# Norm weights, positions and conv taps: five transposes on TensorE against two block transposes on VectorE

## The reference

```python
def rmsnorm(x, gain):
    xf = x.astype(jnp.float32)
    y = xf * lax.rsqrt(jnp.mean(xf * xf, axis=-1, keepdims=True) + EPS)
    return (y * gain.astype(jnp.float32)).astype(x.dtype)

def swiglu(x, w1, w3, w2):
    return (jax.nn.silu(x @ w1) * (x @ w3)) @ w2

# block 1
h = h + 0.5 * swiglu(rmsnorm(h, ffn1_norm), ffn1_w1, ffn1_w3, ffn1_w2)     # D_FF = 2816
u = rmsnorm(h, mix_norm);  proj = u @ w_in                                 # then pooling and retention
a = pool_mixer(u_pool, pool_w, pool_scale);  b = retention(q, k, v, g, ret_norm)
h = h + jnp.concatenate([a, b], axis=-1) @ w_out
h = h + 0.5 * swiglu(rmsnorm(h, ffn2_norm), ...);  x = rmsnorm(h, final_norm)
# block 2: rmsnorm (norm_mix), window and compressed attention (adds cmp_pos_k, cmp_pos_v to the keys
# and values), rmsnorm (norm_ffn), then a feed-forward whose 5632 inner columns go through a causal
# convolution over 3 tokens (conv_w, conv_b), then rmsnorm (norm_final)
```

## Time and profile before

| | |
|---|---|
| median of 3 runs | 834.4 us (834.33 to 834.74) |
| the profiled execution | 834.21 us, its span 832.4 us |
| TensorE busy | 823.4 us, 99% of the span |
| VectorE, ScalarE, GpSimd busy | 625.1, 439.5, 89.8 us (75%, 53%, 11%) |
| DMA, mean over the span | 189 GB/s |

### The profile page before, as it was taken

One profiled execution on the slowest core, in us unless ns is written; L12 is line 12 of the kernel. 1 busy time (PEld: TensorE's weight loads), 2 busy tenths in 40 slices (PEclk: granted clock), 3 DMA queues, 4 the chain that ended last, 5 costly groups with the idle time before them and its releaser, 6 DMA issues.

```text
span 832.4 us, 13214 instructions
## 1 busy us (share of the span) xinstructions
PE 823.4 (99%) x5041; PEld 711.0 (85%) x5041; DVE 625.1 (75%) x779; ACT 439.5 (53%) x559; POOL 89.8 (11%) x93
## 2 busy tenths in 40 slices
PE   9999999999999999999999999999999999999996
PEld 6888888888988888888888899878788988888895
DVE  5786766667977587667667779767874898998897
ACT  6555444546334554454444746566435556665664
POOL 0300000004450300000000317000003000000001
PEclk9999999999999999999999999999999999999999
DMA  8876566564844458756665594684545365466551
GB/s 260 304 239 213 188 194 204 170 201 151 254 153 151 152 185 259 246 194 201 198 205 152 130 243 125 175 259 150 177 157 181 118 204 200 151 206 216 183 176 52
DMA packets 115888, 157.69 MB, mean 189 GB/s; under 512 B 4445, under 2 KB 95997, under 8 KB 115725
## 3 DMA queue, kind: packets, MB, share of 16 engines
q1 hardware_dynamic: 113212, 150.56, 56.3%
q0 software_dynamic: 1392, 5.34, 1.9%
q10 hardware_dynamic: 1248, 1.32, 0.5%
HBM read 154.42 MB, written 1.07 MB: 187 GB/s over the span
## 4 chain that ended last, share of the span: by engine, by line
PE 96%; DVE 1%; DMA 1%; ACT 1%; issue 1%; POOL 0%; ACTq 0%; POOLq 0%; DVEq 0%
PE wk L1760 30%; PE acc L1882 20%; PE wk L1729 16%; PE wk L1768 16%; PE acc L1859 7%; PE acc L2173 1%; PE acc L1776 1%; PE wk L2209 1%; PE acc L1729 1%; DMA x<-in_x 1%; PE acc L2188 1%; PE wk L2246 0%; ACT w_hi L516 0%; PE acc L1895 0%; DVE w_lo L1061 0%
## 5 line engine op out<-in xcount | busy, mean ns | idle before, releaser
L1760 PE MATMUL wk<-xhl,w_hi 128*128 128x512 f32 x1104 | 268.9, 391 | 0.0
L1078 DVE TENSOR_TENSOR w_lo<-raw,w_hi 128x2048 fp32r<-128x2048 f32 x83 | 189.9, 2289 | 63.7 <-ACT w_hi L523 62.5
L1760 PEld LDWEIGHTS wk<-xhl,w_hi 128*128 128x128 f32 x1104 | 202.3, 188 | 39.3 <-issue 0.3
L523 ACT ACTIVATE w_hi<-raw 128x2048 fp32r<-128x2048 f32 x83 | 158.0, 1903 | 0.0
L1768 PEld LDWEIGHTS wk<-xhl,w_lo 128*128 128x128 f32 x1104 | 145.5, 191 | 8.0
L1768 PE MATMUL wk<-xhl,w_lo 128*128 128x256 f32 x1104 | 147.9, 282 | 0.0
L516 ACT ACTIVATE w_hi<-raw 128x2048 fp32r<-128x2048 f32 x51 | 97.0, 1911 | 53.7 <-PE wk L1729 28.4
L1061 DVE TENSOR_TENSOR w_lo<-raw,w_hi 128x2048 fp32r<-128x2048 f32 x44 | 101.3, 2302 | 24.9 <-ACT w_hi L516 24.7
L1882 PE MATMUL acc<-w_hi,hhl 128*128 128x512 f32 x480 | 119.4, 391 | 0.0
L1882 PEld LDWEIGHTS acc<-w_hi,hhl 128*128 128x128 f32 x480 | 88.2, 188 | 17.1
L1729 PE MATMUL wk<-xhl,w_hi 128*128 128x256 f32 x352 | 61.3, 286 | 0.0
(11 more groups left out here) (266 smaller groups left out, 977.9 us busy)
## 6 DMA issues: line engine op xcount, KB each, us to landing
raw<-in_ffn_w SPq DMA_DIRECT2D x64, 1024.0 KB, 5.3
raw<-in_w_in SPq DMA_DIRECT2D x24, 1024.0 KB, 7.2
raw<-in_w_ffn_in SPq DMA_DIRECT2D x22, 1024.0 KB, 5.0
raw<-in_w_ffn_out SPq DMA_DIRECT2D x11, 1024.0 KB, 4.9
raw<-in_w_out SPq DMA_DIRECT2D x8, 1024.0 KB, 4.9
arena<-bias_scratch POOLq DMA_DIRECT2D x4, 512.0 KB, 6.2
raw<-in_w_in SPq DMA_DIRECT2D x4, 512.0 KB, 7.0
raw<-in_cmp_w_k SPq DMA_DIRECT2D x2, 1024.0 KB, 5.5
```

The source lines that it names most:

```text
L523: nc.scalar.activation(w_hi[:, s], raw[:, s], ACT.Copy).then_inc(hi_done, 1)
L1078: nc.vector.tensor_tensor(w_lo[:, s], raw[:, s], w_hi[:, s].bitcast(F32), ALU.subtract) \
L1760: mm = nc.tensor.matmul(bank, wh[:, c, cols], xhl[:, c].rearrange("p n t -> p (n t)"), start=c == 0, stop=False, skip_group_check=True)
```

## The change

Four things:

1. `small_loads` on SyncE's queue loses its 14 small loads. GpSimd's queue gets them in quarters: 32 columns at a time and at most 32 rows, each to the partitions 32j to 32j+31 of `quarter_rows`, which GpSimd sets to zero first. That is 4 quarters of 10 vectors, and 4 quarters of 2 pieces (32 and 12 rows) of 4 taps: 72 loads of 4 to 32 rows of 128 bytes, 1056 rows in all. They stand on GpSimd's queue behind the table and `pool_w`, and ahead of the product of the two norm weights.
2. TensorE's five transposes and ScalarE's two copies go, with their waits.
3. VectorE turns the quarters in blocks of 32 by 32: one instruction over 96 columns to `vec`, one over 256 columns to `conv`. They stand in the last step of the first feed-forward, between the remainder of that step's last weight unit and `b_add`.
4. ScalarE waits for `vec_ready` ahead of the scaling that follows the first feed-forward. `conv` has 64 instead of 44 columns per tap.

```diff
@@ small_loads (SyncE)
-                for col, name in ((V_MIX, "mix_norm"), (V_FFN2, "ffn2_norm"), (V_MIX2, "norm_mix_2"),
-                                  (V_FFN3, "norm_ffn_2"), (V_POOL, "pool_scale"), (V_RET, "ret_norm")):
-                    v = rows8(a[name][0])
-                    sp.dma_start(vec_rows[col:col + v.shape[0], :], v).then_inc(vec_in, 16)
...
-                for j in range(3):
-                    sp.dma_start(conv_rows[:, j], rows8(a["conv_w_2"][0, j])).then_inc(conv_in, 16)
-                sp.dma_start(conv_rows[:, 3], rows8(a["conv_b_2"][0])).then_inc(conv_in, 16)
@@ ScalarE
+                if n == 1:
+                    act.wait_ge(vec_ready, 2)
                 for c in range(DC):
                     x_hi(c, n, gain)
...
-                    vectors()
@@ GpSimd
+            nc.gpsimd.memset(quarter_rows, 0.0).then_inc(rows_zero, 1)
...
             nc.gpsimd.dma_start(scratch, bias_rows).then_inc(bias_written, 16)
+            nc.gpsimd.dma_start(table, a["c_table"]).then_inc(table_in, 16)
+            nc.gpsimd.dma_start(pool_ws, a["pool_w"][0].rearrange("g k n -> k g n")).then_inc(pw_in, 16)
+
+            def quarters(at, rows):
+
+                n = rows.shape[0]
+                for r0 in range(0, n, 32):
+                    m, (block, first) = min(32, n - r0), divmod(at + r0, 32)
+                    for j in range(4):
+                        nc.gpsimd.dma_start(quarter_rows[32 * j + first:32 * j + first + m, 32 * block:32 * block + 32],
+                                            rows[r0:r0 + m, 32 * j:32 * j + 32]).then_inc(vec_in, 16)
+
+            pool.wait_ge(rows_zero, 1)
...
             pool.wait_ge(vec_ready, 2)
             nc.gpsimd.tensor_tensor(vec[:, V_BOTH:V_COLS], vec[:, V_FINAL:V_FINAL + DC], vec[:, V_MIX2:V_MIX2 + DC],
                                     ALU.mult).then_inc(both_gain, 1)
-            nc.gpsimd.dma_start(table, a["c_table"]).then_inc(table_in, 16)
-            nc.gpsimd.dma_start(pool_ws, a["pool_w"][0].rearrange("g k n -> k g n")).then_inc(pw_in, 16)
@@ VectorE, last step of ffn
                 lo(base + 3 * FI - 1)
+                if f == 0:
+                    dve.wait_ge(vec_in, 16 * VEC_LOADS)
+                    nc.vector.transpose(vec[:, 0:R_CONV], quarter_rows[:, 0:R_CONV]).then_inc(vec_ready, 1)
+                    nc.vector.transpose(conv[:].rearrange("p j f -> p (j f)"), quarter_rows[:, R_CONV:]) \
+                        .then_inc(vec_ready, 1)
                 b_part(FI - 1)
@@ TensorE
                     if spreads:
                         pe.wait_ge(rstd_ready, n + 1)
-                        pe.wait_ge(vec_ready, 2)
...
-                    turn_vectors()
```

More of the change, by code:

```diff
@@ L114 @@
 V_BOTH, V_COLS = 96, 104
+R_CONV, R_COLS = 96, 96 + 4 * 64
+VEC_LOADS = 4 * (10 + 2 * 4)
 C_ID, C_FOLD, C_VALC, C_BLK, C_COLS = 0, 128, 160, 190, 198
@@ L213, in build @@
         vec_rows = carve(8, P)
+        quarter_rows = carve(9, R_COLS)
         q_s, k_s = carve(0, HR, T), carve(4, HR, T)
@@ L237, in build @@
         bias_table = carve(57.5, NBUCKET)[0:16]
-        conv_rows = carve(58, 4, P)[0:44]
         bias = carve(0, 16, T)
@@ L264, in build @@
         wg_raw = work[:, 5, T:T + 192].rearrange("p (k n) -> p k n", k=DC)
-        conv = sb("conv", [P, 4, 44])
+        conv = sb("conv", [P, 4, 64])
         sink = sb("sink", [P, NHA])
@@ L307, in build @@
         const_set = sem("const_set")
-        vec_turned, vec_ready = sem("vec_turned"), sem("vec_ready")
+        rows_zero, vec_ready = sem("rows_zero"), sem("vec_ready")
         acc_ready, x_ready, turned, xh_ready, xl_ready, sq_ready = (
@@ L329, in build @@
             sem(n) for n in ("gate_tanh", "head_out", "head_hi", "head_lo"))
-        bias_in, conv_in, cw2_in, wg_in, sink_in = (
-            sem(n) for n in ("bias_in", "conv_in", "cw2_in", "wg_in", "sink_in"))
+        bias_in, cw2_in, wg_in, sink_in = (
+            sem(n) for n in ("bias_in", "cw2_in", "wg_in", "sink_in"))
         bias_set, bias_written, bias_ready = (sem(n) for n in ("bias_set", "bias_written", "bias_ready"))
@@ L619, in ffn @@
                 hi(base + 3 * FI + 1)
[L621 to L626, removed]
             for p in range(4):
@@ L933, in _ @@
             nc.gpsimd.dma_start(scratch, bias_rows).then_inc(bias_written, 16)
+            nc.gpsimd.dma_start(table, a["c_table"]).then_inc(table_in, 16)
[8 more added lines that the diff above has]
+            pool.wait_ge(rows_zero, 1)
+            for col, name in ((V_MIX, "mix_norm"), (V_FFN2, "ffn2_norm"), (V_MIX2, "norm_mix_2"),
+                              (V_FFN3, "norm_ffn_2"), (V_POOL, "pool_scale"), (V_RET, "ret_norm")):
+                quarters(col, rows8(a[name][0]))
+            for col, name in ((V_FINAL, "final_norm"), (V_FINAL2, "norm_final_2")):
+                quarters(col, rows8(a[name]))
+            for col, name in ((V_POSK, "cmp_pos_k_2"), (V_POSV, "cmp_pos_v_2")):
+                quarters(col, a[name][0].rearrange("(j s) d -> j (s d)", s=2))
+            for j in range(4):
+                quarters(R_CONV + 64 * j, rows8(a["conv_w_2"][0, j] if j < 3 else a["conv_b_2"][0]))
             pool.wait_ge(vec_ready, 2)
@@ L2017, in second_unit @@
                 return split_low(slot, 1, wk[:, 3])
[L2019 to L2027, removed]
             pe.wait_ge(const_set, 3)
```

## The result

The changed kernel takes 838.88 us (median of 5 runs, 838.78 to 839.19) against 834.4 us before (834.33 to 834.74): ratio 1.0051, 95% interval 1.004 to 1.0062. It is slower by 4.5 us, 0.5%. The prediction said 834.9 us, within 833.9 to 836.2. Its profiled execution has a span of 836.9 us. In all the sets of this document one execution, of the kernel with one added load, ran at a lower granted clock (0.75) and took 1018.3 us; it is in no comparison.

What follows compares the result with a forecast made beforehand. The prediction took TensorE's work and waits as the bound. Terms: 0 (transposes), 0 (ScalarE, SyncE, GpSimd, traffic) and 0.50 (VectorE) made +0.5 us, 834.7 from the profiled 834.21, or 834.9 against the median; range 833.9 to 836.2 us.

Steps and rivals of the forecast that it cites:

- What bounds the kernel: Whole program: TensorE, busy 823.4 of 832.4 us, so the total moves only with TensorE's work or its waits.
- the 0 for GpSimd in the sum: GpSimd's queue: issuing the 72 loads from about 30 us stays hidden and adds 0 us to the total.
- The transposes that go: TensorE between units 1 and 2, near 20 us: removal gains 0 us, bounds 0 and -0.45 us.
- Rival A: TensorE, unit 1 to unit 2: it recovers the transposes' 0.45 us, total 834.4 to 834.5 us; chance 8%.
- The block transposes: VectorE ahead of `b_add`, end of the first feed-forward: +0.50 us fully on the path, bounds 0.31 and 1.60 us.
- rival B: VectorE, end of the first feed-forward: a block transpose costs four passes, +1.6 us, total 836.0 us; chance 7%.
- The 72 loads on GpSimd's queue: GpSimd from about 30.2 us: issues take 37 to 62 us, hidden before VectorE needs them at 182.9; 0 us.
- rival C: VectorE's wait at 182.9 us: the quarters come too late; at 2.5 us a load, total 862 us; chance 4%.
- SyncE's queue: SyncE, near 10 to 16 us: unit 3's load goes out up to 6.4 us earlier, nobody waits; 0 us.
- rival D: Near 16 us: unit 3's load shares the DMA with unit 2's, up to +6.3 us, 834.9 to 841.2; chance 4%.

## Why the prediction was wrong

**What bounds the kernel: the failed step.** The prediction said that "The total moves only where TensorE's work changes, or where a wait of TensorE appears or goes". That holds as long as TensorE works, up to about 826 us. The execution ends with the last engine's closing drain, and GpSimd's had 832.2 - 830.0 = 2.2 us to spare before. The term that failed is the 0 for GpSimd in the sum. I counted what 72 loads cost where they are issued and where they are waited for, and not what they leave on the queue for the end: 72 x 0.082 = 5.9 us, of which 3.7 stood out. The kernel with the 72 loads alone and the one with the inserted drain show it: +3.8 us and -3.5 us. The rows for it existed in the trace of before, a drain of 2.35 us on GpSimd against 0.007 on SyncE. The busy times and the timeline leave drains out; they stand in the list of the instructions of the program's last line, which the prediction did not use. They would have shown the drain and its room; what one load more costs could not be read there, since there was only the one number of loads, 20.

**The transposes that go, 0 us: right.** The wait for the remainder took their place. I expected unit 2 at 20.6 to 20.7 us behind 0.4 us of idle time; in the profile after, unit 2 landed later and it is

```profile
21.04 1.68 PEld L1770 LDWEIGHTS wk<-xhl,w_hi 128*128 128x128 f32 x8 [0.99 <-issue]
```

Rival A falls by the run with five idle transposes.

**The block transposes, +0.50 us: right.** 0.27 and 0.40 us each, from start to start 183.27 - 183.08 = 0.19 and 183.60 - 183.27 = 0.33, together 0.52. The timeline after, against the earlier trace rows:

```profile
183.08 0.27 DVE L1220 STREAM_TRANSPOSE vec<-arena 128x96 f32<-128x96 f32 x1
183.27 0.40 DVE L1221 STREAM_TRANSPOSE conv<-arena 128x256 f32<-128x256 f32 x1
183.60 0.65 DVE L1164 TENSOR_TENSOR work<-wk,work 128x512 f32<-128x512 f32 x1
...
187.75 0.19 PEld L1869 LDWEIGHTS acc<-w_hi,mhl 128*128 128x128 f32 x1 [0.86 <-issue]
```

The idle time ahead of the closing unit grew from 0.38 to 0.86, so 0.48 us reached TensorE. A transpose streams like an elementwise operation here; rival B falls.

**The 72 loads on GpSimd's queue, 0 us: right for the place, wrong for the total.** They took 0.48 to 0.54 us each to issue, from 30.37 to 65.95 us, just under the lower of my bounds (37 us in all), and VectorE did not wait. So rival C falls. The figure of 3.1 us a load from the Trainium skill ("SBUF — State Buffer", "SBUF: two separate sides") was not put to the test: the page ties it to a mode of VectorE that takes both ports, and every VectorE operation between 30 and 66 us here has two inputs.

**SyncE's queue: 0 us, not excluded.** Unit 3 went out at 12.21 instead of 16.31 us and nobody gained. Unit 2 began 0.39 us later on TensorE (21.04 against 20.65), of which 0.19 was left at 180.87 us. The copy of unit 2 began at 16.61 us instead of 16.21, which I had named as the sign of rival D. Its 6.3 us are out, and holding unit 3 back did not change the time measurably. Whether the 0.2 us belong to it stays open.

The sum by the profile: 0.48 (block transposes) + 0.27 (the rest of the 0.75, of which 0.19 are the opening) + 3.7 (closing drain) = 4.45 us, against 4.5 by the spans.

## What to carry to other kernels

Ahead of an estimate, look at what every engine does between the last computation and the end of the span, and how much room each closing drain has; a load moved to GpSimd's queue took that engine's time twice here, 0.5 us at its issue and 0.082 at the next drain. Where many small loads must go over that queue, a drain in a stretch in which GpSimd idles takes their backlog off the end (838.88 to 835.34 us here). And before work is removed from the busiest engine, read which wait stands directly behind it: here it had to be loosened before the removal was worth anything.

## What the runs showed of the hardware that was not expected

- GpSimd's drain takes 0.082 us for each load issued since the last drain, about 0.1 us besides, and the wait for GpSimd's last operation, 0.6 us at the closing one: 2.35, 2.43, 4.31, 5.29 and 8.23 us at 20, 21, 44, 56 and 92 loads, whatever their size and however long they had landed, and 2.02 us at 16 after an inserted drain. "Load" counts every transfer that GpSimd issues, its few stores too. The Trainium skill ("VectorE: DVE Perf Modes", "The DRAIN you can't avoid") gives about 12 ns, constant, for the drains that belong to a program's frame on all five engines; that is near SyncE's 7 ns here and does not fit GpSimd's.
- A float32 block transpose on VectorE, 128 partitions, is listed with 0.27 us for 96 columns and 0.40 for 256; from start to start it took 0.19 and 0.33.
